# Moving four small steps of a gated-delta head loop: state products in two blocks, P on ScalarE, X ahead of the decays, z copied bank by bank

## The chip, the cores and the metric

The kernel runs on one NeuronCore of a Trainium2 chip. The metric is the device time of one execution in microseconds (us), lower is better. Before the change it is 2142.4 us, the median of three runs (2137.96, 2142.4 and 2145.52). The profiled execution is a fourth one, of 2137.08 us.

## The reference, cut to what matters

One step of a two-layer decoder over 320 tokens: 256 of a new prompt and 8 sequences with 8 new tokens each. Layer 1 is a gated DeltaNet mixer, layer 2 a pooling mixer; the change touches layer 1 alone. Its core, for 16 key heads with two value heads each:

```python
proj = h @ w_in                                   # 2048 x 12352: q, k, v, z, gates
qkv, conv_new = causal_conv(qkv, conv_buf, conv_w)   # width 4, then silu
q = l2norm(q) * HEAD_DIM ** -0.5;  k = l2norm(k)
# in chunks: S_t = exp(g_t) S_{t-1};  S_t += beta_t k_t (v_t - S_t^T k_t)^T;  o_t = S_t^T q_t
lmat = einsum('cd,ed->ce', kb, k) * decay_strict
tmat = triangular_solve(lmat + eye, eye)          # (1 + L)^-1, unit lower triangular
u = tmat @ (v * beta) - (tmat @ (kb * exp(gc))) @ s
o = (q * exp(gc)) @ s + (qk * decay_incl) @ u
s = s * exp(g_last) + kdec.T @ u
out = (rmsnorm(o, o_norm_w) * silu(z)) @ w_out
```

## The kernel before, in words

Everything is float32. A projection product is made of three fp32r matmuls: each weight and each activation is split into a high part (ScalarE, line 282, `whi`) and a remainder (VectorE, line 287, `wlo`), and `k_tile` (lines 290 to 298) multiplies high by high, high by low and low by high. A call of `k_tile` handles one tile of 128 rows of the inner dimension for two blocks of 128 output columns: six matmuls with 320 columns. A piece of weights has 4 such tiles; four slots hold pieces, SyncE loads them.

Layer 1 runs as a loop over heads with a software pipeline. Turn i does the attention-like work of head i-1 (`delta`, in each engine's part) and, between its many small products, the projection of head i: 48 tiles in three jobs of 16, job 0 for q and k (PSUM banks 0 and 1), job 1 for v (banks 2 and 3), job 2 for z (banks 0 and 1 again). TensorE's small products go to banks 4 to 7, named D0 to D3. Where TensorE's code says `fill(n)`, n projection tiles are issued: they are there to cover the time in which another engine answers. There is no scheduler. The order on each engine is the order of the code; engines meet at semaphores (`wait_ge`, `then_inc`). The loop has 15 turns (i from 1 to 15), and the sixteenth head runs behind it with tiles of the output projection as fill.

The inverse (1 + L)^-1 is built by doubling. Level k (1 to 5, `TILE_LEVELS`) makes two products, both in 32 x 32 blocks: one of L and Y (its end is `lp{k}`), which another engine copies out of PSUM as P (`pc`, or `p5` at level 5), and one of X and P (`lxt`), which ScalarE copies out as Y (`yc`, ended by `y{k}`), and VectorE turns into X (`xc`, line 1037). Level 5 joins 16 to 32 rows, a sixth level 32 to 64 (`p6`, `ym`, ended by `lp6`, `xt6`, `y6`). Y's full form `ym` is put together by GpSimd (line 551) once `y4` is there. GpSimd also scales the states (line 549) after the state products. The state products (line 1317) are 64 matmuls of 128 x 32 weights (`kq_m`, masked k and q) with the cached states `s_s` of the 8 sequences; they go to D3.

Beside that VectorE runs the convolution of head i (`conv_next`, line 937), the exponents of the next head's decays (`decays_next`, line 946), and the splits. ScalarE copies the projections out of PSUM: `qk_evac`, `v_evac` (lines 627 and 628), `z_evac` (line 635, into `zraw`), and saves the convolution's last rows (`cc_tail`, line 652). In the loop `v_evac` and `cc_tail` follow the eighth split, at level 4. At the end of a turn TensorE turns the head's output (`turned`, line 1290) and the next turn's first fill may start only when z has been copied, since it writes banks 0 and 1. The engines also wait for each other's round marks at the head of `delta` (`rounds`).

## Time and profile before

| | |
|---|---|
| three runs | 2137.96, 2142.4, 2145.52 us |
| profiled execution, its span | 2137.08 us, 2135.4 us |
| TensorE busy | 97% of the span, 19533 matmuls |
| VectorE, ScalarE, GpSimd busy | 1317.4, 842.4, 252.1 us |
| granted clock, mean | 0.99 |
| DMA | 311.40 MB, 146 GB/s |

Times of rows are microseconds from the start of the span, durations of one instruction are in ns where a row says mean. A busy TensorE is not one at its peak, since the ends of matmuls are modelled and matmuls overlap: the distance of two starts says what a matmul costs, not its duration. The clock is the share that was granted, 1.00 for 2.4 GHz. The head loop lies between about 111 and 1065 us.

### The profile page before, as it was taken

What the parts mean: (1) busy time and instruction counts of PE and PEld (TensorE: products, weight loads), DVE (VectorE), ACT (ScalarE), POOL (GpSimd) and SP (SyncE); (2) the same over time, 40 slices, a digit from 0 to 9 for tenths busy, and PEclk for the clock granted to TensorE, in tenths of its full rate; (3) what the DMA queues carried; (4) which work ended last, traced back from release to release, by engine and by line L of the source; (5) the groups of instructions that cost most, each with busy time, mean ns of one, the idle gap of its engine ahead of it and who ended that gap; (6) DMA issues with size and microseconds to landing.
All of it is one profiled execution on the core that took longest, in us unless ns stands there. A gap on an engine that the chain in (4) does not pass through costs nothing.

```text
span 2135.4 us, 51389 instructions
## 1 busy us (share of the span) xinstructions
PE 2073.1 (97%) x19533; PEld 1980.2 (93%) x19533; DVE 1317.4 (62%) x2203; ACT 842.4 (39%) x1674; POOL 252.1 (12%) x354
## 2 busy tenths in 40 slices
PE   6999999999999999999999999999999999999998
PEld 4889998989999999998889999999999999999997
DVE  4567777666777677677755444555555556654443
ACT  3444443434444434444443333433333333333333
POOL 3022121121121222112110010000000000000010
PEclk9999999999999999999999999999999999999999
DMA  5545544455453455545356445544444454444442
GB/s 162 148 117 148 148 141 129 118 149 148 133 163 113 134 163 146 153 132 150 117 156 192 138 143 173 158 146 149 159 154 146 155 162 156 146 152 150 157 140 88
DMA packets 379995, 311.40 MB, mean 146 GB/s; under 512 B 19609, under 2 KB 375866, under 8 KB 379322
## 3 DMA queue, kind: packets, MB, share of 16 engines
q1 hardware_dynamic: 378042, 306.30, 47.5%
q10 hardware_dynamic: 1872, 3.96, 0.5%
q8 instruction: 58, 0.95, 0.2%
q14 instruction: 23, 0.19, 0.0%
HBM read 283.85 MB, written 27.25 MB: 146 GB/s over the span
## 4 chain that ended last, share of the span: by engine, by line
PE 90%; DVE 5%; issue 3%; ACT 1%; DMA 0%; DVEq 0%; SPq 0%; ACTq 0%
PE ps L296 27%; PE ps L298 25%; PE ps L297 25%; PE ps L1153 8%; PE ps L1317 1%; DVE wlo L287 1%; DVE dec L946 1%; DVE convout L937 1%; PE ps L1174 1%; DMA xtok<-in_x_sample_dram 0%; ACT zraw L635 0%; DVE sq L843 0%; PE ps L1223 0%; PE ps L1267 0%; DVE s_s L1086 0%
## 5 line engine op out<-in xcount | busy, mean ns | idle before, releaser
L296 PE MATMUL ps<-xhi,whi 128*128 128x320 f32 x3072 | 995.1, 324 | 16.9 <-ACT zraw L635 7.4
L298 PE MATMUL ps<-xhi,wlo 128*128 128x320 f32 x3072 | 954.6, 311 | 2.3 <-issue 2.3
L297 PE MATMUL ps<-xlo,whi 128*128 128x320 f32 x3072 | 954.2, 311 | 2.7 <-issue 2.7
L287 DVE TENSOR_TENSOR wlo<-wraw,whi 128x1024 fp32r<-128x1024 f32 (+1 forms) x484 | 615.6, 1293 | 230.7 <-ACT whi L282 228.0
L296 PEld LDWEIGHTS ps<-xhi,whi 128*128 128x128 f32 x3072 | 581.4, 189 | 41.0 <-issue 32.9
L282 ACT ACTIVATE whi<-wraw 128x1024 fp32r<-128x1024 f32 (+1 forms) x484 | 495.6, 1049 | 262.6 <-PE ps L298 236.7
L298 PEld LDWEIGHTS ps<-xhi,wlo 128*128 128x128 f32 x3072 | 580.6, 189 | 6.0 <-issue 6.0
L297 PEld LDWEIGHTS ps<-xlo,whi 128*128 128x128 f32 x3072 | 581.8, 189 | 0.8
L298 PE MATMUL ps<-bhi,wlo 128*128 128x320 f32 x512 | 158.2, 309 | 0.0
L297 PE MATMUL ps<-blo,whi 128*128 128x320 f32 x512 | 158.2, 309 | 0.0
L296 PE MATMUL ps<-bhi,whi 128*128 128x320 f32 x512 | 158.1, 309 | 0.0
L1486 POOL TENSOR_TENSOR sacc<-sacc,sqp 128x640 f32<-128x640 f32 x12 | 18.9, 1575 | 942.9 <-ACT sqp L1509 942.9
L937 DVE SCALAR_TENSOR_TENSOR convout<-convin,cwcur,convout 128x344 f32<-128x344 f32 x192 | 102.0, 573 | 0.0
L1565 DVE TENSOR_TENSOR ht<-ps,ht 128x640 f32<-128x640 f32 x29 | 23.9, 825 | 122.3 <-PE ps L298 86.8
L298 PEld LDWEIGHTS ps<-bhi,wlo 128*128 128x128 f32 x512 | 96.2, 188 | 0.0
L296 PEld LDWEIGHTS ps<-bhi,whi 128*128 128x128 f32 x512 | 96.2, 188 | 0.0
L297 PEld LDWEIGHTS ps<-blo,whi 128*128 128x128 f32 x512 | 96.2, 188 | 0.0
L992 DVE SCALAR_TENSOR_TENSOR lmat<-ps,cur,dec 128x128 f32<-128x128 f32 x80 | 22.2, 344 | 101.4 <-PE ps L1153 101.4
L296 PE MATMUL ps<-phi,whi 128*128 128x320 f32 x256 | 78.9, 308 | 0.0
L297 PE MATMUL ps<-plo,whi 128*128 128x320 f32 x256 | 78.9, 308 | 0.0
L298 PE MATMUL ps<-phi,wlo 128*128 128x320 f32 x256 | 78.9, 308 | 0.0
L728 ACT ACTIVATE yc<-ps 128x64 f32<-128x64 f32 (+1 forms) x48 | 11.0, 229 | 159.2 <-PE ps L1153 159.2
(338 smaller groups left out, 2171.9 us busy)
## 6 DMA issues: line engine op xcount, KB each, us to landing
wraw<-in_delta_w_in_dram SPq DMA_DIRECT2D x384, 256.0 KB, 3.2
wraw<-in_pool_w_in_dram SPq DMA_DIRECT2D x256, 256.0 KB, 3.1
wraw<-in_delta_w_out_dram SPq DMA_DIRECT2D x128, 256.0 KB, 3.3
wraw<-in_pool_w_out_dram SPq DMA_DIRECT2D x128, 256.0 KB, 3.2
s_s<-in_state_delta_dram SPq DMA_DIRECT2D x32, 512.0 KB, 6.3
out_dram<-s_s SPq DMA_DIRECT2D x32, 512.0 KB, 5.0
wraw<-in_pool_w_group_dram SPq DMA_DIRECT2D x64, 256.0 KB, 3.1
dec<-gc_rows SPq DMA_DIRECT2D x16, 320.0 KB, 5.0
```

What stands on the lines that cost most here:

```text
L282: nc.scalar.activation(whi[:, slot, 0:width], wraw[:, slot, 0:width], ACT.Copy).then_inc(E("w_hi"), 1)
L287: nc.vector.tensor_tensor(wlo[:, slot, 0:width], wraw[:, slot, 0:width], whi[:, slot, 0:width].bitcast(F32), ALU.subtract).then_inc(E("w_l ...
L296: mm(o, whi[:, slot, w], hi[:, k_x, :], start=first, stop=False)
L297: mm(o, whi[:, slot, w], lo[:, k_x, :], start=False, stop=False)
L298: done = mm(o, wlo[:, slot, w], hi[:, k_x, :], start=False, stop=last)
L937: ins = v.scalar_tensor_tensor(convout[:, q, :], convin[:, q, j:j + CV], cwcur[:, q, j:j + 1], convout[:, q, :], ALU.mult, ALU.add)
L946: last = v.scalar_tensor_tensor(dec[:, u, :], dec[:, u, :], gc_next[:, u:u + 1], mask_p[:] if u < 4 else mask_s[:], ALU.add, ALU.add)
L992: last = v.scalar_tensor_tensor(lmat[:, u, :], D0[:, P * (u % 2 if u < 4 else 2):P * (u % 2 if u < 4 else 2) + P], cur[:, NBETA + u:NBETA ...
L1153: return mm(out, lhsT, rhs, start=True, stop=True)
L1174: mm(ps[:, 0, 0:T], ones[:], sq[:, q % 4, :], start=q == 0, stop=False).then_inc(E("sq_used"), 1)
L1317: last = mm(D3[32 * j:32 * j + 32, 256 + P * m:384 + P * m], kq_m[:, at:at + 32], s_s[:, 4 * h + b, q, :], start=b == 0, stop=b == 3)
L1565: v.tensor_tensor(tiles, ps[:, 2 * (j % 2):2 * (j % 2) + 2, 0:T], tiles, ALU.add).then_inc(E(f"free{j % 2}"), 1)
```

## The change

Four things, all in layer 1.

1. State products (TensorE): the one block of 64 at level 2, behind the fill of that level, becomes two of 32 (`states_part`): one behind the X-P product of level 1, one behind that of level 2. There they stand in the place of `fill(1)`. The two tiles go to the fills ahead of the X-P products, and one more tile goes there from the fill of 8 ahead of the normalized keys, which becomes 7.
2. P of level 5: ScalarE instead of VectorE copies it (`p5`), and then does its eighth split. The copy of v moves from level 4 behind the level-5 copy of Y, the convolution's last rows behind P6.
3. X: VectorE turns Y of level 4 before it computes the next head's decay exponents, not after. The copies of X into `xm` still come behind these, and the eighth split on VectorE behind the third such copy. TensorE waits for `x4` by name, since P no longer comes from the same engine.
4. z: the last two tiles of job 2 are multiplied bank by bank, with a signal (`z_half`) when bank 0 is complete, and ScalarE copies each bank when it is complete. For head 0 z is now copied within `silus`, ahead of the sample copies.

```diff
-    def k_tile(slot, k_w, hi, lo, k_x, pair, first, last):
+    def k_tile(slot, k_w, hi, lo, k_x, pair, first, last, halves=(0, 1)):
...
-        for h in range(2):
+        for h in halves:
...
         def z_evac(i, used):
-            act.wait_ge(E("w_used"), used)
+            act.wait_ge(E("z_half"), i + 1)
             if loop_of(i):
                 act.wait_ge(E("gate"), i)
-            sc.activation(zraw[:], ps[:, 0:2, 0:T], ACT.Copy).then_inc(E("z_evac"), 1)
+            sc.activation(zraw[:, 0, :], ps[:, 0, 0:T], ACT.Copy)
+            act.wait_ge(E("w_used"), used)
+            sc.activation(zraw[:, 1, :], ps[:, 1, 0:T], ACT.Copy).then_inc(E("z_evac"), 1)
...
-            if loop_of(i):
-                z_evac(i, i * 12 + (HEADS + 12))
+            z_evac(i, i * 12 + (HEADS + 12))
             act.wait_ge(E("silu"), i + 1)
...
+                if k == TILE_LEVELS:
+                    act.wait_ge(E("lp5"), n)
+                    sc.activation(p5[:], blocks(D0[:, 0:P], 4), ACT.Copy).then_inc(E("p5"), 1)
+                    split(8)
                 act.wait_ge(E("lxt"), (n - 1) * 5 + k)
...
-                if k < 5:
+                if k < 4:
                     split(4 + k)
+            v_next()
             act.wait_ge(E("lp6"), n)
             sc.activation(p6[0:64, :, :], blocks(D0[0:64, 0:256], 4), ACT.Copy).then_inc(E("p6"), 1)
+            tail_next()
             split(9)
...
         silus(0)
-        z_evac(0, HEADS + 12)
...
-                if j == 8:
-                    v_evac(i, i * 12 + (HEADS + 8))
-                    cc_tail(i)
...
-                    v.tensor_copy(p5[:], blocks(D0[:, 0:P], 4)).then_inc(E("p5"), 1)
                     dve.wait_ge(E("x4"), n)
...
-                if k == 4:
-                    decays_next()
                 if k < TILE_LEVELS:
                     dve.wait_ge(E("c_all"), 1)
                     dve.wait_ge(E(f"y{k}"), n)
                     turned = v.transpose(xc[:, 0:units, :], yc[:, 0:units, :])
                     if k == TILE_LEVELS - 1:
                         turned.then_inc(E("x4"), 1)
+                        decays_next()
...
-                last = k_tile((p // PK) % 4, k % PK, xhi, xlo, k, job % 2, k == 0, k == KT - 1)
+                slot = (p // PK) % 4
+                if job < 2 or k < KT - 2:
+                    last = k_tile(slot, k % PK, xhi, xlo, k, job % 2, k == 0, k == KT - 1)
+                elif k == KT - 1:
+                    for h in range(2):
+                        for kk in (KT - 2, KT - 1):
+                            last = k_tile(slot, kk % PK, xhi, xlo, kk, job % 2, False, kk == KT - 1, (h,))
+                        if h == 0:
+                            last.then_inc(E("z_half"), 1)
...
-            fill(8)
+            fill(7)
...
+            def states_part(part):
+
+                if part == 0:
+                    pe.wait_ge(E("kq_m"), n)
+                    pe.wait_ge(E("state_landed"), n * 32)
+                for b in range(4):
+                    for j in range(4):
+                        h, q = j % 2, j // 2
+                        at = (2 * part + h) * P + 32 * b
+                        last = mm(D3[32 * j:32 * j + 32, 256 + P * part:384 + P * part], kq_m[:, at:at + 32],
+                                  s_s[:, 4 * h + b, q, :], start=b == 0, stop=b == 3)
+                if part == 1:
+                    last.then_inc(E("ksqs_ps"), 1)
...
-                fill((2, 1, 2, 3, 2)[k - 1])
-                if k == 2:
...
-                    last.then_inc(E("ksqs_ps"), 1)
+                fill((3, 2, 3, 3, 2)[k - 1])
                 x = x0 if k == 1 else xc
                 pe.wait_ge(E("ident"), 1)
+                if k == TILE_LEVELS:
+                    pe.wait_ge(E("x4"), n)
                 pe.wait_ge(E(f"p{k}"), n)
...
-                if k < TILE_LEVELS:
+                if k < 3:
+                    states_part(k - 1)
+                elif k < TILE_LEVELS:
                     fill(1)
```

On TensorE, in the loop at levels 1 to 3, the rows before, from the L-Y product of level 2 to that of level 3 (`xhi,whi` and its two like are a fill tile's matmuls):

```order
L1153 MATMUL ps<-yc,lmat 32x16 [waits y1,ident]
L1153 MATMUL ps<-yc,lmat 32x16 x19
L296 MATMUL ps<-xhi,whi 128x320
...
L1317 MATMUL ps<-s_s,kq_m 32x128 [waits state_landed]
L1317 MATMUL ps<-s_s,kq_m 32x128 x31
L1153 MATMUL ps<-pc,xc 32x16 [waits p2,ident]
L1153 MATMUL ps<-pc,xc 32x16 x19
L296 MATMUL ps<-xhi,whi 128x320
...
L1153 MATMUL ps<-yc,lmat 32x16 [waits y2,ident]
```

and in the changed kernel, from the X-P product of level 1 to the L-Y product of level 3:

```order
L1156 MATMUL ps<-pc,x_100 32x32 [waits p1,ident]
L1156 MATMUL ps<-pc,x_100 32x32 x19
L1310 REGISTER_ALU [waits kq_m]
L1315 MATMUL ps<-s_s,kq_m 32x128 [waits state_landed]
L1315 MATMUL ps<-s_s,kq_m 32x128 x15
L1156 MATMUL ps<-yc,lmat 32x16 [waits y1,ident]
...
L1156 MATMUL ps<-pc,xc 32x16 [waits p2,ident]
L1156 MATMUL ps<-pc,xc 32x16 x19
L1315 MATMUL ps<-s_s,kq_m 32x128 x16
L1156 MATMUL ps<-yc,lmat 32x16 [waits y2,ident]
```

A state block now stands directly between two small products, without a fill on either side.

On VectorE, in the loop at levels 4 and 5, before (`p_82` is P of level 5, `dec` the decays of the next head):

```order
L1014 COPY_PREDICATED pc<-level,ps 128x4x16 [waits lp4,c_all]
...
L946 SCALAR_TENSOR_TENSOR dec<-dec,gc_next,mask_p 128x128 [waits hidden,dec_landed]
L946 SCALAR_TENSOR_TENSOR dec<-dec,gc_next,mask_p 128x128 x3
L946 SCALAR_TENSOR_TENSOR dec<-dec,gc_next,mask_s 128x128
L1037 STREAM_TRANSPOSE xc<-yc 128x128 [waits y4,c_all]
L1018 COPY p_82<-ps 128x128 [waits lp5,c_all]
L1020 COPY xm<-xc 32x4x32 [waits x4]
```

and in the changed kernel:

```order
L1018 COPY_PREDICATED pc<-level,ps 128x4x16 [waits lp4,c_all]
...
L1038 STREAM_TRANSPOSE xc<-yc 128x128 [waits y4,c_all]
L947 REGISTER_ALU
L950 SCALAR_TENSOR_TENSOR dec<-dec,gc_next,mask_p 128x128 [waits hidden,dec_landed]
L950 SCALAR_TENSOR_TENSOR dec<-dec,gc_next,mask_p 128x128 x3
L950 SCALAR_TENSOR_TENSOR dec<-dec,gc_next,mask_s 128x128
L1023 COPY xm<-xc 32x4x32 [waits x4]
```

The turning of X has passed the five exponents, and P's copy has left the engine.

On ScalarE, at the same place, before (`p_92` is P6):

```order
L728 ACTIVATE yc<-ps 128x4x16 [waits lxt]
L281 REGISTER_ALU [waits w_landed2]
L282 ACTIVATE whi<-wraw 128x1024 [waits w_used]
L627 ACTIVATE convin<-ps 128x2x256 [waits conv,w_used]
L628 ACTIVATE convin<-ps 128x2x8x8
L652 ACTIVATE tail<-convin 128x4x24 [waits v_evac,qk_evac,cc_o]
L654 ACTIVATE tail<-convin 128x4x3
L729 REGISTER_ALU
L732 ACTIVATE ym<-ps 32x4x32 [waits ym,lxt]
L732 ACTIVATE ym<-ps 32x4x32
L737 ACTIVATE p_92<-ps 64x256 [waits lp6]
```

and in the changed kernel:

```order
L733 ACTIVATE yc<-ps 128x4x16 [waits lxt]
L727 ACTIVATE p_82<-ps 128x128 [waits lp5]
L281 REGISTER_ALU [waits w_landed2]
L282 ACTIVATE whi<-wraw 128x1024 [waits w_used]
L729 REGISTER_ALU
L737 ACTIVATE ym<-ps 32x4x32 [waits ym,lxt]
L737 ACTIVATE ym<-ps 32x4x32
L627 ACTIVATE convin<-ps 128x2x256 [waits conv,w_used]
L628 ACTIVATE convin<-ps 128x2x8x8
L743 ACTIVATE p_92<-ps 64x256 [waits lp6]
L654 ACTIVATE tail<-convin 128x4x24 [waits v_evac,qk_evac,cc_o]
```

The copies of v (`convin`) now lie between the Y copies of level 5 and P6, and the tail behind P6.

## Rows read from the trace of the kernel before

**Rows 1.** The page, busy time of each engine over the span.

```profile
PE 2073.1 (97%) x19533; PEld 1980.2 (93%) x19533; DVE 1317.4 (62%) x2203; ACT 842.4 (39%) x1674; POOL 252.1 (12%) x354
```

**Rows 2.** Who waited for whom, TensorE: us in total, times, longest.

```profile
PE ps L296 <- ACT zraw L635: 7.4, 13, 3.5
PE ps L1153 <- DVE p L1018: 7.0, 13, 0.6
PE ps L296 <- issue: 5.8, 2, 3.0
```

**Rows 3.** Timelines of SyncE and TensorE (start, us, instruction), and the states' tile.

```profile
506.48 1.03 SPq L347 DMA_DIRECT2D s_s<-in_state_delta_dram  x2
...
526.76 0.41 PE L296 MATMUL ps<-xhi,whi 128*128 128x320 f32 x1
...
527.84 1.95 PE L1317 MATMUL ps<-s_s,kq_m 128*32 128x128 f32 x64
529.72 0.53 PE L1153 MATMUL ps<-pc,xc 32*32 32x16 f32 x40
...
531.62 0.41 PE L296 MATMUL ps<-xhi,whi 128*128 128x320 f32 x1
...
533.57 0.44 PE L1153 MATMUL ps<-pc,xc 32*32 32x16 f32 x32
...
L1317 PE MATMUL ps<-s_s,kq_m x64: 272/273/297, 527.8 to 529.5; 128*32 128x128 f32 x64
```

**Rows 4.** Three turns by window: length, engines busy, granted clock, DMA share, GB/s.

```profile
300.41:363.03 62.62, 61.73 (x773) 57.05 (x771) 46.28 (x93) 27.28 (x72) 13.01 (x12) 1.00 0.50 144
363.03:433.13 70.10, 64.49 (x774) 59.28 (x773) 45.13 (x93) 27.33 (x72) 12.80 (x12) 0.95 0.46 130
433.13:501.03 67.90, 63.62 (x773) 58.59 (x771) 46.21 (x93) 27.27 (x72) 13.25 (x12) 0.97 0.47 134
```

**Rows 5.** Timelines of ScalarE, GpSimd, VectorE and TensorE at levels 4 and 5.

```profile
538.73 0.22 ACT L728 ACTIVATE yc<-ps 128x64 f32<-128x64 f32 x1 [3.46 <-PE ps L1153]
...
539.03 1.82 POOL L551 TENSOR_TENSOR ym<-yc,blocks 128x640 f32<-128x640 f32 x1 [4.60 <-ACT yc L728]
...
539.37 2.43 DVE L946 SCALAR_TENSOR_TENSOR dec<-dec,gc_next,mask_p 128x128 f32<-128x128 f32 x4
...
541.98 0.30 DVE L1037 STREAM_TRANSPOSE xc<-yc 128x128 f32<-128x128 f32 x1
...
542.61 0.34 PE L1153 MATMUL ps<-p,xc 32*32 32x32 f32 x11 [0.56 <-DVE p L1018]
```

**Rows 6.** ScalarE's timeline from the copy of v to P6.

```profile
541.20 0.60 ACT L627 ACTIVATE convin<-ps 128x512 f32<-128x512 f32 x1 [1.30 <-PE ps L298]
541.69 0.28 ACT L628 ACTIVATE convin<-ps 128x128 f32<-128x128 f32 x1
...
544.91 0.38 ACT L737 ACTIVATE p<-ps 64x256 f32<-64x256 f32 x1 [1.28 <-PE ps L1153]
```

**Rows 7.** Timelines of TensorE and ScalarE at the end of a turn.

```profile
501.03 0.71 PE L1290 MATMUL ps<-ident,amat 128*128 128x128 f32 x5
...
501.23 0.70 ACT L635 ACTIVATE zraw<-ps 128x640 f32<-128x640 f32 x1 [4.37 <-PE ps L298]
...
502.06 0.41 PE L296 MATMUL ps<-xhi,whi 128*128 128x320 f32 x1 [0.33 <-ACT zraw L635]
```

**Rows 8.** Timelines ahead of the loop's first turn, and the window behind it.

```profile
106.86 0.76 ACT L679 ACTIVATE silu<-convout 128x688 f32<-128x688 f32 x1
...
109.12 0.86 DVE L960 SCALAR_TENSOR_TENSOR silu<-silu,convout 128x688 f32<-128x688 f32 x1
...
110.63 0.68 ACT L635 ACTIVATE zraw<-ps 128x640 f32<-128x640 f32 x1
...
111.45 0.41 PE L296 MATMUL ps<-xhi,whi 128*128 128x320 f32 x1 [3.46 <-ACT zraw L635]
...
111.40:116.60 5.20, 5.15 (x24) 5.16 (x25) 2.69 (x6) 2.53 (x4) 0.15 (x1) 0.67 0.50 147
```

More of the change, by code:

```diff
@@ L690, in branch_hi, with delta @@
             sc.activation(xhi[:, 4 * ch:4 * ch + 4, :], branch[:, 4 * ch:4 * ch + 4, :], ACT.Copy).then_inc(E("b_hi"), 1)
-        def delta(n, split, cached, store, next_silus, begun):
+        def delta(n, split, cached, store, next_silus, begun, v_next, tail_next):
             begun()
@@ L787, in split @@
                     qk_evac(i, i * 12 + (HEADS + 4))
-                if j == 8:
-                    v_evac(i, i * 12 + (HEADS + 8))
-                    cc_tail(i)
-            delta(i, split, lambda i=i: cc_evac(i), lambda i=i: cc_store(i), lambda i=i: silus(i), lambda: None)
+            delta(i, split, lambda i=i: cc_evac(i), lambda i=i: cc_store(i), lambda i=i: silus(i), lambda: None,
+                  lambda i=i: v_evac(i, i * 12 + (HEADS + 8)), lambda i=i: cc_tail(i))
         def out_split(j):
@@ L802, in delta_act @@
         branch_hi(0)
-        delta(NH, out_split, lambda: None, lambda: None, lambda: None, out_begun)
+        delta(NH, out_split, lambda: None, lambda: None, lambda: None, out_begun, lambda: None, lambda: None)
     def delta_dve(dve):
@@ L1010, in delta @@
                 units = 5 if k < S_LEVELS else 4
-                dve.wait_ge(E("c_all"), 1)
-                dve.wait_ge(E(f"lp{k}"), n)
                 if k < TILE_LEVELS:
+                    dve.wait_ge(E("c_all"), 1)
+                    dve.wait_ge(E(f"lp{k}"), n)
                     v.copy_predicated(half_blocks(pc[:, k - 1, 0:units, :], k, 1),
@@ L1021, in delta @@
                     v.tensor_copy(xm[BL:64, :, BL:64], xc[BL:64, 0:4, :])
-                split(3 + k)
-                if k < 5:
+                if k < TILE_LEVELS:
+                    split(3 + k)
                     conv_next(0, k - 1)
@@ L1042, in delta @@
                     v.tensor_copy(xm[BL:64, :, 0:BL], blocks(D2[BL:64, 0:P], 4)).then_inc(E("x5"), 1)
+                    split(8)
             conv_next(1, 0)
@@ L1307, in delta @@
                 last.then_inc(E(f"lp{k}"), 1)
-                fill((2, 1, 2, 3, 2)[k - 1])
-                if k == 2:
-                    pe.wait_ge(E("kq_m"), n)
-                    pe.wait_ge(E("state_landed"), n * 32)
-                    for m in range(2):
-                        for b in range(4):
-                            for j in range(4):
-                                h, q = j % 2, j // 2
-                                at = (2 * m + h) * P + 32 * b
-                                last = mm(D3[32 * j:32 * j + 32, 256 + P * m:384 + P * m], kq_m[:, at:at + 32],
-                                          s_s[:, 4 * h + b, q, :], start=b == 0, stop=b == 3)
-                    last.then_inc(E("ksqs_ps"), 1)
+                fill((3, 2, 3, 3, 2)[k - 1])
                 x = x0 if k == 1 else xc
                 pe.wait_ge(E("ident"), 1)
+                if k == TILE_LEVELS:
+                    pe.wait_ge(E("x4"), n)
                 pe.wait_ge(E(f"p{k}"), n)
```

## The prediction

> **What bounds the kernel now.** I read the page first, then who waited for whom on TensorE, then one turn of the head loop as a timeline, engine by engine. TensorE is busy for 2073.1 us of a span of 2135.4 us [rows 1], so only three things can pay: idle time of TensorE, matmul work that goes away, and time at the lower clock. In the list of waits two of the causes that the change touches stand out: the copy of z out of PSUM (7.4 us in 13 waits, the longest 3.5) and the copy of P at level 5 (7.0 us in 13 waits, never over 0.6) [rows 2]. A third cost is not a wait and stands in no list: what TensorE loses where projection matmuls change to the small matmuls of the heads and back. The timeline of starts shows it. A fill of one projection tile (six matmuls) reaches from 526.76 to 527.84, 1.08 us; one of two tiles from 531.62 to 533.57, 1.95 us [rows 3]. So a tile is worth 0.87 to 0.88 us and a fill costs 0.20 us more for being a piece of its own.
>
> A regular turn takes 62.6 us at full clock; two of the fifteen take 70.1 and 67.9 us [rows 4]. In both TensorE stood about 3 us at the turn with nothing named as releaser (5.8 us in two waits) [rows 2] and then had a lower granted clock (0.95 and 0.97 in the turn's mean).
>
> **State products.** The 64 products go from one block into two of 32. The first start is at 527.8, the last at 529.5, the next small matmul starts at 529.72 [rows 3]: 0.027 us each and some 0.2 us until the following block can start. Two blocks are 2 x (32 x 0.027 + 0.18) = 2.08 us against 1.88, so +0.2 (bounds: 0 if the drain overlaps, 0.4 if a block also has to be entered). Two one-tile fills between the small blocks disappear into longer fills elsewhere: 2 x 0.20 = -0.4. Net -0.2 per head, 16 heads: **-3.3 us** (bounds 0 and -6.4). Each half must cover what the fill covered, the copy of Y by ScalarE. Its like at level 4 starts right after the products end and takes 0.22 us [rows 5]; with 160 columns say 0.3. A half of 1.04 us hides that with about half a microsecond to spare. The fills before P get one tile more, so those covers only grow; the tile comes from the fill of 8, behind which normalized k is long ready. The states are needed about 2.6 us earlier, near 525.2; their loads were issued from 506.48 on [rows 3], over 17 us before, so I take that at 0.
>
> What the Trainium skill says here ("TensorEngine Tiling (Array Packing)", Key Properties): changing the tiling mode, not merely the tile, drains TensorE. The rows agree that there is such a cost, 0.20 us per break. Counted by the rule alone, this stretch has nine changes of mode before and six after, and at half a break each that would be -0.3 per head where my sum has -0.2; it also says that splitting the block is not free, which a count of instructions would miss.
>
> **P of the 16-to-32 level, and X.** In the loop the order on VectorE is: level-4 P, weight split, convolution, exponents of the next head's decays, X turned, P copied. The exponents begin at 539.37 and X is turned only at 541.98, 2.6 us for five instructions, because GpSimd's assembly of Y runs from 539.03 for 1.82 us; then P is copied, and the product starts at 542.61 after 0.56 us of idle TensorE [rows 5]. With the change ScalarE copies P when its product is done (near 540.2) and X is turned at 539.4, when the convolution ends. TensorE's two fill tiles end near 542.0. Both are ready 1.5 us earlier than that, so the wait goes: 7.0 us in all [rows 2], less some 0.3 of the last head, where VectorE is held by a residual addition that stays ahead of X: **-6.7 us** (bounds 0 and -7.0). Decays are now after X and still meet GpSimd; they end near 542 and the copies of X behind them near 542.8, while the product that needs them starts 3 us after the level-5 one. Covered; without cover this would cost at most the 0.6 just won.
>
> ScalarE pays by order: z aside, the v evacuation moves from before the level-5 copy of Y to behind it, ahead of P6. It takes 0.60 + 0.28 us [rows 6]. The Y copy would end near 542.8, v near 543.7, and P6 may start when its product ends, near 544.1 in the new time (before: 544.91 [rows 6], less the 0.8 us won in the turn). So 0.4 us of slack; the tail copy (0.5 us) then goes behind P6 and pushes the next weight split, and Y6 behind it, by about 0.1 us with a fill of one tile as cover. I take 0; if it is not covered it costs up to 0.3 per head, 5 us.
>
> **z bank by bank.** Before, the copy of 640 columns starts at 501.23, 0.70 us long, behind the last z matmul; TensorE has only five transposes from 501.03 and resumes at 502.06 after 0.33 us idle [rows 7]. After, half is copied while the other half is multiplied. A copy of 320 columns lies between 256 (0.38 us) and 512 columns (0.60 us) [rows 6], 0.44 us, so release comes 0.26 us earlier. Twelve clean turns: **-3.2 us** (bounds 0 and 12 x 0.33 = -4.0). The matmuls are the same, only the order of the last two k tiles differs.
>
> The first head has more. There z was copied behind the sample copies, which wait for VectorE's silu (from 109.12): z at 110.63, TensorE resumes at 111.45 after 3.46 us idle, and in the following 5.2 us the granted clock is 0.67, a mix of 2.4 and 1.2 GHz [rows 8]. Now z comes right behind the tanh, which ends at 107.6, and the last z matmul, which ended at 111.45 - 3.46 = 108.0: release near 108.6, -2.8 us. The 24 matmuls of the first fill then took 5.2 us [rows 8] where four tiles of 0.88 are 3.5; with an idle gap of under 1 us, as short as those at which no turn lost clock, this 1.5 us and more should not come. GpSimd's mark of the round, its one instruction of the window, comes after 111.4 [rows 8]; TensorE's fill would end at 108.6 + 3.6 = 112.2, just behind it. Sum **-4.3 us** (bounds -1 if the marks come late, -4.5).
>
> **Sum.** -3.3 - 6.7 - 3.2 - 4.3 = -17.5 us. The profiled execution took 2137.1 us (span 2135.4), giving 2119.6. The other runs are 2138.0, 2142.4 and 2145.5; the difference within these is about one disturbed turn. Off the median of 2142.4 I get 2124.9; off the mean of the four (2140.8) 2123.3. I say 2123.
>
> **Rivals.**
> A, the waits come back as others (chance 0.14): v before P6 or Y6 costs 0.3 per head and the first head stays bound by the round marks. -17.5 + 5 + 3.3 = -9, 2132 us. For it: ScalarE's queue grows denser exactly where TensorE needs four answers within 5 us. Against it: each has slack in the rows as worked out above.
> B, no net gain (0.09): the changes of tile mode around two state blocks cost 0.4 more than I have, and X or P is again late: only z remains, -3 to -5, 2138 us.
> C, slower (0.06): the turn of the loop. TensorE's disturbed turns cost 70.1 - 62.6 = 7.5 and 67.9 - 62.6 = 5.3 us, mean 6.4 [rows 4]. If the moved code makes them more frequent, from 2.7 additional ones (17.5 / 6.4) the gain is gone, from 4 on it is slower by over 0.3%; with five more, 2142.4 - 17.5 + 32 = 2157 us. For it: the same code has both kinds of turn, so it hangs on timing. Against it: the body grows by two instructions on TensorE, and the runs before vary by only one disturbed turn.
> The Trainium skill ("Runtime: NRT & Kernel Launch", Instruction fetch mechanics) says that a taken branch to code outside the fetched window stalls for a fetch. By that rule every turn or none should stall; the trace has it in two of fifteen.
> D, one or both disturbed turns vanish (0.09): 2123 - 6 to - 13, 2110 to 2117 us.
> The forecast itself has 0.62, its own range 2117 to 2129.
>
> **Range and chances.** 2109 to 2137 takes in D and A and part of B. A kernel that runs between 2138 and 2145.5 by itself shows a change of about 0.3% (6.4 us) and more. Faster: 0.62 + 0.14 + 0.09 = 0.85; within 0.3%: 0.09; slower: 0.06.
>
> **What would show it.** In the waits of TensorE the P rows must vanish (no row for P by either engine over 0.1 us) and the z row fall to about 1 us plus under 1 us once. In the timeline a turn takes 62.6 - 0.6 - 0.26 - 0.2 = 61.5 us. The two state blocks take 1.0 to 1.1 us each. The first head loop's F matmuls begin near 108.6, at full clock. Wrong would be: a regular turn of 62.3 us or more, a new wait of TensorE for P6, Y6 or X, VectorE's exponents reaching past the product that needs x5, or more than three turns of 67 us or longer.

## The result, and the profile after

The changed kernel took 2109.3 us (median of six executions, 2104.7 to 2114.2) against 2144.7 us for the kernel before (six executions on the same chip, 2138.0 to 2152.2): ratio 0.983, 95% interval 0.981 to 0.986. The difference of the medians is 35.4 us. I had 2123.0 with a range of 2109 to 2137, a gain of 17.5 to 19.4 us. So the direction was right, the time is at the low end of the range, and the size was half of what these runs show. The profiled executions differ by less, 22.9 us, and that difference can be followed line by line. Five of the executions used below (four of the kernel before, one of the kernel after) are over 1.5% slower than the fastest of their group and count as slow; without them the difference of the means given further down is 29.2 us instead of 27.7.

The page of the kernel after, span and busy times, answers to [rows 1]:

```profile
span 2112.4 us, 51389 instructions
PE 2064.3 (98%) x19533; PEld 1973.4 (93%) x19533; DVE 1335.2 (63%) x2187; ACT 845.7 (40%) x1706; POOL 254.5 (12%) x354
```

TensorE is busy for 8.8 us less. The other 14 us were idle time. Who waited for whom on TensorE (us in total, times, longest), against [rows 2]:

```profile
PE ps L296 <- issue: 5.7, 2, 2.9
PE ps L1650 <- DVE xn L1610: 3.9, 1, 3.9
PE ps L296 <- DVE xlo L956: 3.5, 1, 3.5
```

There is no row for P and none for z any more; only the first row, the wait without a releaser, still stands as before, 5.7 us in two waits.

Turns of the head loop by window (length, engines busy, granted clock of TensorE, DMA share, GB/s), against [rows 4]; the first is a regular one, then the two disturbed ones, then the last head, outside the loop:

```profile
662.66:724.15 61.49, 61.43 (x774) 56.95 (x772) 47.46 (x92) 27.47 (x74) 13.37 (x12) 1.00 0.51 146
724.15:791.93 67.78, 64.57 (x774) 59.60 (x771) 47.06 (x92) 27.47 (x74) 13.01 (x12) 0.95 0.48 134
791.93:860.84 68.91, 63.24 (x773) 58.40 (x771) 46.12 (x92) 27.47 (x74) 13.24 (x12) 0.98 0.46 132
1045.30:1109.78 64.48, 60.67 (x766) 56.39 (x765) 43.81 (x76) 28.94 (x69) 11.07 (x10) 1.00 0.53 167
```

The last head of the kernel before in the same view:

```profile
1064.97:1132.60 67.63, 63.39 (x766) 58.92 (x764) 42.58 (x77) 28.93 (x68) 11.07 (x10) 0.95 0.51 159
```

A regular turn went from 62.62 to 61.49 us. TensorE is idle in it for 0.06 us, where it was for 0.89. "Disturbed" means, here and below, a turn that is over 4 us longer than the regular ones. The 22.9 us of span are made up of

| stretch (start of one turned block to the next) | before | after | difference |
|---|---|---|---|
| up to the first head's turned block | 175.14 | 170.77 | -4.4 |
| twelve regular turns | 12 x 62.65 | 12 x 61.49 | -13.9 |
| two disturbed turns | 70.09 + 67.91 | 67.78 + 68.91 | -1.3 |
| last head | 67.63 | 64.47 | -3.2 |
| everything after it | 1002.8 | 1002.7 | -0.1 |

The three edits can be found one by one in a regular turn, by the distances of starts. From the L-Y product of level 1 to that of level 3 it was 8.90 us and is 8.66 (state products, -0.24). From the L-Y product of level 5 to the product behind it, which waits for P and X, it was 2.96 and is 2.32 (P and X, -0.64). From the turned block to the next fill it was 1.03 and is 0.77 (z, -0.26). Together -1.14 us.

The timeline of TensorE at levels 1 and 2 of the delta inverse (start, us, instruction), against [rows 3]:

```profile
502.14 1.08 PE L1315 MATMUL ps<-s_s,kq_m 128*32 128x128 f32 x32
503.15 0.53 PE L1156 MATMUL ps<-yc,lmat 32*32 32x16 f32 x40
...
506.02 1.08 PE L1315 MATMUL ps<-s_s,kq_m 128*32 128x128 f32 x32
507.03 0.44 PE L1156 MATMUL ps<-yc,lmat 32*32 32x16 f32 x32
```

From the start of a state block to the following product it is 1.01 us each time, 2.02 together for 1.88 in one piece: +0.14, where I had +0.2. The products after them start on the spot, so each half covers the copy of Y.

The timelines of ScalarE, GpSimd, VectorE and TensorE at levels 4 and 5, against [rows 5, 6]:

```profile
515.24 2.38 DVE L941 SCALAR_TENSOR_TENSOR convout<-convin,cwcur,convout 128x344 f32<-128x344 f32 x2
515.39 0.22 ACT L733 ACTIVATE yc<-ps 128x64 f32<-128x64 f32 x1 [3.46 <-PE ps L1156]
515.69 1.56 POOL L551 TENSOR_TENSOR ym<-yc,blocks 128x640 f32<-128x640 f32 x1 [4.42 <-ACT yc L733]
516.80 0.28 ACT L727 ACTIVATE p<-ps 128x128 f32<-128x128 f32 x1 [1.19 <-PE ps L1156]
517.55 0.30 DVE L1038 STREAM_TRANSPOSE xc<-yc 128x128 f32<-128x128 f32 x1
517.78 1.09 DVE L950 SCALAR_TENSOR_TENSOR dec<-dec,gc_next,mask_p 128x128 f32<-128x128 f32 x4
518.64 0.34 PE L1156 MATMUL ps<-p,xc 32*32 32x32 f32 x10
...
519.58 0.58 ACT L627 ACTIVATE convin<-ps 128x512 f32<-128x512 f32 x1
520.05 0.26 ACT L628 ACTIVATE convin<-ps 128x128 f32<-128x128 f32 x1
520.94 0.38 ACT L743 ACTIVATE p<-ps 64x256 f32<-64x256 f32 x1 [0.62 <-PE ps L1156]
```

P stands in SBUF at 517.1 and X is turned at 517.85; the product that needs both starts at 518.64 without a wait. The four exponents of the decays take 1.09 us here and took 2.43 before: GpSimd's assembly (515.69 to 517.25) now lies beside the convolution instead, and that takes 2.38 us where it took 1.05 before:

```profile
538.39 1.05 DVE L937 SCALAR_TENSOR_TENSOR convout<-convin,cwcur,convout 128x344 f32<-128x344 f32 x2
```

So the cost of running beside the assembly was moved, not removed, and X is turned later for it. ScalarE is idle for 0.62 us ahead of P6, so the v copy that was moved there is hidden (I had 0.4 of slack).

ScalarE and TensorE at the end of a turn, against [rows 7]:

```profile
539.01 0.44 ACT L635 ACTIVATE zraw<-ps 128x320 f32<-128x320 f32 x1 [3.49 <-PE ps L298]
539.69 0.71 PE L1301 MATMUL ps<-ident,amat 128*128 128x128 f32 x5
539.89 0.44 ACT L637 ACTIVATE zraw<-ps 128x320 f32<-128x320 f32 x1 [0.44 <-PE ps L298]
540.46 0.41 PE L296 MATMUL ps<-xhi,whi 128*128 128x320 f32 x1
```

The second half of z is copied in 0.44 us, as estimated, and TensorE goes on at 540.46, 0.06 us after its own transposes have ended.

Ahead of the first turn, against [rows 8]: both copies of z and the window of the fill behind them:

```profile
108.29 0.42 ACT L635 ACTIVATE zraw<-ps 128x320 f32<-128x320 f32 x1
...
108.68 0.44 ACT L637 ACTIVATE zraw<-ps 128x320 f32<-128x320 f32 x1
...
107.90:112.50 4.60, 4.11 (x30) 4.03 (x29) 4.22 (x10) 2.94 (x9) 0.15 (x1) 1.00 0.69 194
```

z comes at 109.1 where it came at 111.3, and the fill runs at full clock (1.00) where it had 0.67.

### The profile page after: what moved, and what is told of

The parts are those of the page before. It is cut to its first block, busy times and chain, and to the rows that moved or that the text cites. A ratio compares the mean times of both kernels' runs of the same rounds, so it can differ in the third digit from the quotient of the medians.

```text
span 2112.4 us, 51389 instructions
## 1 busy us (share of the span) xinstructions
PE 2064.3 (98%) x19533; PEld 1973.4 (93%) x19533; DVE 1335.2 (63%) x2187; ACT 845.7 (40%) x1706; POOL 254.5 (12%) x354
## 4 chain that ended last, share of the span: by engine, by line
PE 95%; DVE 3%; issue 1%; DMA 0%; ACT 0%; SPq 0%; DVEq 0%; ACTq 0%
PE ps L296 28%; PE ps L298 26%; PE ps L297 26%; PE ps L1156 9%; PE ps L1315 2%; PE ps L1177 1%; DVE wlo L287 1%; DMA xtok<-in_x_sample_dram 0%; DVE sq L847 0%; PE ps L1301 0%; PE ps L1234 0%; PE ps L1278 0%; DVE s_s L1089 0%; PE ps L1227 0%; DVE xlo L841 0%
## 5 line engine op out<-in xcount | busy, mean ns | idle before, releaser
L287 DVE TENSOR_TENSOR wlo<-wraw,whi 128x1024 fp32r<-128x1024 f32 (+1 forms) x484 | 628.0, 1319 | 228.2 <-ACT whi L282 225.7
L941 DVE SCALAR_TENSOR_TENSOR convout<-convin,cwcur,convout 128x344 f32<-128x344 f32 x192 | 118.5, 659 | 0.0
```

The source lines that it names most:

```text
L287: nc.vector.tensor_tensor(wlo[:, slot, 0:width], wraw[:, slot, 0:width], whi[:, slot, 0:width].bitcast(F32), ALU.subtract).then_inc(E("w_l ...
L941: ins = v.scalar_tensor_tensor(convout[:, q, :], convin[:, q, j:j + CV], cwcur[:, q, j:j + 1], convout[:, q, :], ALU.mult, ALU.add)
```

## The experiments

There were twelve runs, in three groups, of eleven kernels (e4 and e8 repeat the two kernels compared, e12 repeats e7); the kernels of a group share the runs of the kernel before on their chip. "Level 5" below is the 16-to-32 level; turn times are read as above, from one turned block of TensorE to the next.

**e1: z as before.** The rest of the change stays.

```diff
         def z_evac(i, used):
-            act.wait_ge(E("z_half"), i + 1)
+            act.wait_ge(E("w_used"), used)
             if loop_of(i):
                 act.wait_ge(E("gate"), i)
-            sc.activation(zraw[:, 0, :], ps[:, 0, 0:T], ACT.Copy)
-            act.wait_ge(E("w_used"), used)
-            sc.activation(zraw[:, 1, :], ps[:, 1, 0:T], ACT.Copy).then_inc(E("z_evac"), 1)
+            sc.activation(zraw[:], ps[:, 0:2, 0:T], ACT.Copy).then_inc(E("z_evac"), 1)
...
```

> The changed kernel with z as before: one copy of 640 columns, no order by bank, and z of head 0 behind the sample copies. Theory 1 (the parts are worth what the steps of the prediction give, and what is measured above their sum comes from turns of the head loop in which TensorE stalls about 3 us at the jump back, 6 to 7.5 us each, and whose number differs from execution to execution): a clean turn is 61.49 + 0.27 = 61.75 us, the first head about 4.3 us longer, so +7.5 us on the changed kernel's 2109: 2117. Theory 2 (the parts interact, each saves more than its term): +12 us or more, with a clean turn above 61.9 us.

Measured: 2118.1 us (2108.4 to 2128.4, six), ratio to before 0.988 (0.983 to 0.993). Trace: regular turn 61.80 us, 0.31 more than with the change; the first turned block at 174.57 instead of 170.77. TensorE's waits have the row again:

```profile
PE ps L296 <- ACT zraw L635: 6.7, 13, 2.8
```

So z is worth 0.3 us per turn, as worked out, and some 4 us once; the second is less sure, since the first turned block of the unaltered changed kernel lay at 170.77 us in one trace and at 168.29 in the other (e4).

**e2: P, X, decays, v and tail copy as before.** The rest of the change stays.

```diff
-                if k == TILE_LEVELS:
-                    act.wait_ge(E("lp5"), n)
-                    sc.activation(p5[:], blocks(D0[:, 0:P], 4), ACT.Copy).then_inc(E("p5"), 1)
...
                 else:
+                    v.tensor_copy(p5[:], blocks(D0[:, 0:P], 4)).then_inc(E("p5"), 1)
...
+                if k == 4:
+                    decays_next()
```

> The changed kernel with P of level 5 copied by VectorE, X turned behind the decays' exponents, and the copies of v and of the convolution's last rows at their old places. Theory 1: a clean turn is 61.49 + 0.6 = 62.1 us, in all +7 us, 2116. Theory 2: +12 us or more; the other parts had brought the small products closer together, so that the wait would now be longer than the 0.6 us of before.

Measured: 2115.9 us (2109.6 to 2127.0), ratio 0.987 (0.983 to 0.991). Trace: regular turns 61.93 to 62.16 us, 0.44 to 0.67 more, and the waits show P:

```profile
PE ps L1154 <- DVE p L1019: 5.4, 13, 0.5
```

**e3: one state block as before.**

```diff
+                if k == 2:
+                    pe.wait_ge(E("kq_m"), n)
+                    pe.wait_ge(E("state_landed"), n * 32)
+                    for m in range(2):
...
-                if k < 3:
-                    states_part(k - 1)
-                elif k < TILE_LEVELS:
+                if k < TILE_LEVELS:
                     fill(1)
```

> The changed kernel with one block of 64 state products at level 2 and the fills as before. Theory 1: a clean turn is 61.49 + 0.2 to 0.3 = 61.7 to 61.8 us, +3 to +4 us, 2113. Theory 2: +8 us or more.

Measured: 2113.4 us (2103.8 to 2119.8), ratio 0.986 (0.982 to 0.990). Trace: regular turn 61.73 us, 0.24 more (I had 0.2). This trace has one disturbed turn, 68.88 us.

**e4: the change again, unaltered**, as the measure for the three above.

> The changed kernel once more, unchanged, as the mark for the three others and for a second trace of it. Theory 1: a clean turn is again 61.49 us, but the number or the place of the turns of 67 us and more differs from the first trace (turns 10 and 11 there), and the time moves with it. If the place and number are the same as in the first trace, what disturbs them is not chance and theory 1 has to be changed.

Measured: 2113.2 us (2099.3 to 2142.4), ratio 0.986 (0.981 to 0.992). The trace's regular turn is 61.47 us. Disturbed are the sixth and the tenth turn (67.35, 68.63); in the first trace of the same kernel they were the tenth and the eleventh:

```profile
414.17:475.64 61.47, 61.41 (x773) 56.94 (x772) 47.46 (x92) 27.52 (x74) 13.07 (x12) 1.00 0.51 146
475.64:542.99 67.35, 63.04 (x773) 58.07 (x772) 46.63 (x92) 27.51 (x74) 13.03 (x12) 0.97 0.47 135
```

The three parts, taken back one at a time, cost 0.31, 0.44 to 0.67 and 0.24 us of a turn, 0.99 to 1.22 together; the change as a whole won 1.14. They add up and don't hide one another. In the medians of six (2118.1, 2115.9, 2113.4, 2113.2) the order is the expected one but e3 can't be told from e4, and the six executions of e4 alone spread over 43 us (28 without the slowest).

**e5 and e6: TensorE's loop over the heads written out**, in the kernel after and in the one before. It takes away the jump back at the end of a turn, and leaves each turn's work as it is.

```diff
...
-        with pe.Fori(1, NH) as i:
+        for i in range(1, NH):
```

> The changed kernel with TensorE's head loop written out: its 15 turns stand one behind another, without a jump back; the other engines keep their loops, the work and the waits are the same. Theory 1 (the stalls of about 3 us belong to TensorE's jump back): no turn of over 63 us, all turns 61.5 us, the time 2100 us (the profiled span of 2112.4 less 6.3 and 7.4 us of its two disturbed turns, plus 1.7), and the executions lie within some 6 us of each other instead of 40. Rival (the stalls come from what TensorE waits for at a turn, z or the round marks, or from DMA traffic): disturbed turns stay as frequent. Rival 2: code now has to be fetched for every turn, and each turn gets its own short stalls, as in the first turn: all turns 1 us or more longer, 2115 us or more.

Measured e5: 2118.3 us (2111.7 to 2122.1), ratio 0.989 (0.985 to 0.993). No turn begins with a stall (the starts of the last transpose and of the next fill are 0.25 us apart at each), but turns take 61.39 to 65.17 us. So the stalls of about 3 us went with the jump back, as theory 1 had it, but the time is that of rival 2: TensorE has short stalls within the turns, and fourteen turns take 14.8 us more than at 61.39 us each. Three of them, and the rows of the DMA queue that brings code and of the waits:

```profile
168.01:233.18 65.17, 63.41 (x774) 58.67 (x772) 47.47 (x92) 27.50 (x74) 13.14 (x12) 0.97 0.50 139
...
298.24:360.96 62.72, 61.61 (x774) 57.04 (x772) 47.34 (x92) 27.51 (x74) 13.30 (x12) 1.00 0.50 144
360.96:422.35 61.39, 61.39 (x774) 56.92 (x771) 47.48 (x92) 27.51 (x74) 13.19 (x12) 1.00 0.52 147
...
q8 instruction: 126, 2.06, 0.4%
...
PE ps L1156 <- issue: 5.0, 7, 1.3
PE ps L1315 <- issue: 4.7, 4, 1.8
```

> The kernel before with TensorE's head loop written out in the same way. Theory 1: clean turns of 62.6 us throughout, 2124 us, and so a distance of 24 us to the changed kernel without its jump back; that distance is then what the four edits are worth, and the rest of the 35 us between the first medians is a different number of disturbed turns. If the distance stays at 30 us or more, the edits themselves are worth more than the traces show.

Measured e6: 2130.4 us (2127.8 to 2136.4, twelve), ratio 0.995 (0.992 to 0.997). Turns 62.56 to 66.23 us. The spread over twelve executions is 8.7 us, where the looped kernel before spread over 35 us in 23 executions of the same job, and over 38 us in the twelve of e8. That shows where most of the spread comes from: the jump back. The written-out loop trades the 3 us stall for short ones within the turns.

The two written-out kernels are only 12.1 us apart by their medians, where 24 were expected, and 17.0 us in the traces (spans 2127.0 and 2110.0). Their undisturbed turns differ as before, 62.56 and 61.39 us, but the short stalls cost the changed kernel more: 14.8 us over fourteen turns against 9.0. The trace of e5 is its fastest execution (2111.7 us), so in the others the stalls may have cost more still; no trace shows it. What the change is worth thus depends on how the loop's code is fetched, and 24 us hold for the looped kernels alone.

**e7: TensorE waits for z bank by bank too.** In the change ScalarE copies by banks but TensorE waits for both.

```diff
-            sc.activation(zraw[:, 0, :], ps[:, 0, 0:T], ACT.Copy)
+            sc.activation(zraw[:, 0, :], ps[:, 0, 0:T], ACT.Copy).then_inc(E("z_first"), 1)
...
-                if job < 2 or k < KT - 2:
+                if job == 0 and k == 0 and not isinstance(i, int):
+                    k_tile(slot, 0, xhi, xlo, k, 0, True, False, (0,))
+                    pe.wait_ge(E("z_evac"), i)
+                    last = k_tile(slot, 0, xhi, xlo, k, 0, True, False, (1,))
+                elif job < 2 or k < KT - 2:
```

> The changed kernel with z released to TensorE bank by bank: the first product of the next turn waits for the copy of bank 0 only, and for bank 1 only ahead of its second half. In the trace of the changed kernel 0.30 us of a turn are still lost behind the turned output (starts 0.33 us apart where 0.03 is the least). Theory: the distance falls to 0.03, a clean turn to 61.2 us, 15 turns make -4.5 us, the first head about -0.4 more: 2105 to 2108 by median, in the clean turns -0.3. Rival: the wait between the two halves costs as much as it saves, a clean turn stays at 61.5 us.

Measured: 2096.1 us (2094.6 to 2113.4), ratio 0.979 (0.975 to 0.983), the lowest of all and below the 2105 to 2108 expected (the same kernel gave 2105.3 in e12). The trace's regular turn is 61.16 us, with the gap between the transposes and the next fill down to 0.03 us:

```profile
307.85:369.01 61.16, 61.16 (x774) 56.92 (x772) 47.49 (x92) 27.50 (x74) 13.02 (x12) 1.00 0.52 146
```

**e8: the kernel before, unaltered**, twelve executions.

> The kernel before once more, for a second trace. Theory 1: clean turns of 62.6 us as in the first, another number or place of turns of 67 us and more; over its executions the number must be 3 or so in the mean, since the median lies some 20 us above the 2124 of a run without any.

Measured: 2143.2 us (2125.5 to 2163.8), ratio 0.998 (0.995 to 1.002). The trace (span 2149.8) has three disturbed turns, 72.05, 71.81 and 69.69 us, and its regular turn is 62.63 us as ever. What queue q8 carried, first for the kernel before in the first trace (two disturbed turns), then here (three), then for e3 (one):

```profile
q8 instruction: 58, 0.95, 0.2%
```

```profile
q8 instruction: 67, 1.10, 0.2%
```

```profile
q8 instruction: 49, 0.80, 0.2%
```

That is 40 packets and nine more for each disturbed turn. It held in all twelve traces of looped kernels: 49 with one, 58 with two, 67 with three, and one packet more (59 with two, 68 with three) in the two kernels below that have 128 matmuls more ahead of the loop. In the first trace of before the stretch of a disturbed turn, 363.03 to 433.13, has

```profile
q8 instruction: 9, 0.15, 1.0%
```

and a regular one (563.66 to 626.29) has no such row. So a disturbed turn is one in which code is fetched again; that it is TensorE's loop body follows from e5, where TensorE's loop alone is written out and no turn begins with the stall.

**e9: the kernel before with head 0's z copied early**, nothing else.

```diff
-            if loop_of(i):
-                z_evac(i, i * 12 + (HEADS + 12))
+            z_evac(i, i * 12 + (HEADS + 12))
...
-        z_evac(0, HEADS + 12)
```

> The kernel before with one edit: z of head 0 is copied ahead of the sample copies instead of behind them. Theory (the prediction's step): TensorE idles some 0.9 us ahead of the loop instead of 3.0 to 3.7, loses no clock there, and the first turn's output comes 3.5 to 4.3 us earlier; later turns stay at 62.63 us. About 2138 us by mean, if the number of disturbed turns stays the same as before. Rival: the round marks or the loads of the first weights hold the first head, and it gains under 1 us.

Measured: 2142.6 us (2120.1 to 2151.6, twelve), ratio 1.002 (0.999 to 1.005). In the trace TensorE resumes 1.0 us after its last start instead of 3.7 and the first turned block is at 171.74, 3.4 us earlier than in the first trace of the kernel before and 4.6 earlier than in e8. The local gain is there, but the times don't show it: the median is 4.7 us above that of the 29 executions of the kernel before in this job (2138.0), the mean 4.3 above (2141.1 and 2136.8). This trace has three disturbed turns (69.66, 71.57, 70.31).

**e10: a shift by 64 one-column products ahead of the loop**, in the kernel before. If the place of the loop's code, or the moment at which the loop starts, decided how many turns are disturbed, this would change their number. In the trace each of the 64 calls has become two matmuls with a weight load each, so there are 128 more matmuls (19661), not 64.

```diff
         pe.wait_ge(E("cc_out"), 1)
+        for _ in range(64):
+            one(D2[:, 0:1], ident[:], ones[:, 0:1])
         one(D2[:, 0:1], ident[:], ones[:, 0:1]).then_inc(E("pe_round"), 1)
```

> The kernel before with 64 matmuls of one column, with their 64 weight loads, ahead of TensorE's head loop. They compute nothing that is used and lie in a stretch where TensorE waits for z anyway; they move the loop's code by 128 instructions. Theory (where the code lies sets how often the jump back ends in a stall): the number of disturbed turns changes clearly, the spread of the executions (2125 to 2165 so far, 0 to 6 disturbed turns of 6.5 us) becomes narrow, at 2124 to 2128 or above 2150. Rival (it is chance from one execution to the next, whatever the place): mean 2144, spread of 20 us or more, as without the shift.

Measured: 2163.1 us (2145.3 to 2181.6, twelve), ratio 1.011 (1.007 to 1.015). It looks like three more disturbed turns, and the trace says otherwise: there are three, as in e8, but the first turned block is at 193.82 us instead of 175.14. The added matmuls themselves, and the stretch at the lower clock:

```profile
106.58 22.89 PE L1153 MATMUL ps<-ones,ident 128*128 128x1 f32 x130
...
111.90:132.40 20.50, 20.50 (x95) 20.50 (x95) 2.19 (x6) 0.90 (x2) 0.15 (x1) 0.50 0.17 52
```

The one-column matmuls (130, with the two of the round mark that were there before) run without a pause from 106.58 to 129.3 us, 0.11 us from start to start until the granted clock falls at 111.9, and 0.21 us after that. The first fill begins at 129.34 instead of 111.45. So they did not fit into the wait for z, and the 18.7 us by which the first turned block is late are nearly all their own time. Less that, the median is 2144.4 us; e8's is 2143.2, the 29 executions of the kernel before in this job have 2138.0.

**e11 and e12: the same shift in the kernel of e7, and that kernel again.**

```diff
+        for _ in range(64):
+            one(D2[:, 0:1], ident[:], ones[:, 0:1])
```

> The kernel with z released bank by bank (clean turns of 61.16 us) with the same 64 small matmuls ahead of the loop. They do not all fit into the wait there, so up to 1.5 us are lost in the first head. Theory of the place of the code: another number of disturbed turns than without the shift (0 in four of six executions there), so 2096 or below with hardly a disturbed one, or 2110 and above. Rival (chance): as without the shift, most executions at 2096 to 2098 and one or two 6 to 13 us above.

Measured e11: 2133.3 us (2122.5 to 2148.1, twelve), ratio 0.998 (0.995 to 1.001). First turned block at 192.28, 24.3 us later than in e12 and 20.7 later than in e7 (171.61); the one-column matmuls again run from 106.61 to 129.4 us. Two disturbed turns. Neither of the two times expected, 2096 or 2110 and above, allowed for the some 20 us that the added matmuls take.

> The kernel with z released bank by bank once more. If the number of disturbed turns of a kernel is fixed by its code, it again has few: median 2095 to 2099. If it is chance, the executions spread over 2095 to 2120 as those of the changed kernel do (2099 to 2142), with clean turns of 61.16 us all the same.

Measured e12: 2105.3 us (2101.4 to 2129.2, six), ratio 0.987 (0.983 to 0.991). The trace (span 2099.6) has one disturbed turn. The same stretch as above, without the shift:

```profile
111.90:132.40 20.50, 20.50 (x279) 19.82 (x280) 12.89 (x33) 9.61 (x32) 3.53 (x6) 1.00 0.44 130
```

e7 and e12 are one kernel; their medians differ by 9 us and their regular turns by nothing (61.16). That the place of the code or the loop's starting moment sets the number of disturbed turns is not borne out by e10 and e11: their traces have three and two with the shift, as those without have three or two, and two or one. These are counts of one trace each.

## Why the prediction was right or wrong

**Right: the mechanisms, and what each is worth in a turn.** The P wait is gone, with P ready 1.5 us ahead of the product as I had it. X is ready only 0.8 us ahead, where I had 1.5 for it too: I expected GpSimd's assembly to meet the decays still, and it met the convolution ahead of X (2.38 us for 1.05). e2 prices this part at 0.44 to 0.67 us per turn for 0.56 to 0.6 forecast. Two state blocks cost 0.14 instead of 0.2, and e3 prices the part at 0.24 for 0.2. e1 prices z at 0.31 for 0.26. ScalarE's v, P6 and Y6 cost nothing, as forecast. The first head came 4.4 us earlier for 4.3, and both of its terms are in the trace: the distance of starts at the gap went from 3.71 to 0.74 us, and the clock of the fill from 0.67 to 1.00. That the sum fits to 0.1 us is luck: the same two kernels in e8 and e4 have their first turned block at 176.38 and 168.29 us, 8.1 apart. A regular turn takes 61.49 us where I wrote 61.5.

On the drain: that changing the tiling mode drains TensorE (the Trainium skill, "TensorEngine Tiling (Array Packing)", Key Properties) agrees with the rows. A block of 32 state products goes from its last start to the following product in 0.2 us, in two blocks as in one. But I counted the changes of mode wrong. From the L-Y product of level 1 to that of level 3 there are nine before and eight after, not six (31 and 30 over a whole turn). At half a break each that is -0.1 per head, where this stretch became 0.24 us shorter and e3 gives 0.24. The count of pieces did better: two fills of their own less, 2 x 0.20, and 0.14 more for the second state block, make -0.26.

**Wrong: the size of the sum.** Where it was short shows in the table above. First, the last head: my terms left it 0.3 us. Its stretch had another cost before that I hadn't read, TensorE idle for 4 us ahead of the fill and then a lower clock (0.95 over the stretch). After, the stall is nearly the same (3.99 and 3.78 us) but in this execution no clock was lost: -3.2. In the other traces of kernels with the change it was lost in part (65.95 us in e4, 66.52 in e2), and 64.47 is the lowest of the eight traces of looped kernels with the change (the others 65.95 to 66.94), where the four with the old code have 66.91 to 67.88. So half or more of the 3.2 is luck of the trace. Second, the three terms make 1.02 us of a regular turn (0.56 + 0.26 + 0.2), 12.2 over twelve, and they measured 13.9, 1.7 more: the P term most of all, for the list of waits holds only the 0.56 us of idle time and the stretch became 0.64 shorter; a few of the regular turns before were also up to 0.12 us longer than 62.63. Third, the disturbed turns together gave 1.3 for some 0.5; they vary by more than that from one to the next. That is 2.9 + 1.7 + 0.8, the 5.4 us between 17.5 and 22.9.

**Wrong: the step from one execution to the medians.** "The difference within these is about one disturbed turn", taken from four executions, was the step that failed most, and with it the choice to weigh rivals C and D at 0.06 and 0.09. Taking each trace's disturbed turns down to regular ones leaves 2135.4 - 12.7 = 2122.7 us of span before and 2112.4 - 13.7 = 2098.7 after, 24.0 apart (as times, with the 1.7 us around the span, 2124.4 and 2100.4). The second pair of traces, e8 and e4, gives 2124.2 and 2097.7 us of span in the same way, 26.5 apart. The times of 81 executions of the kernel before run from 2121.0 to 2164.7, the lowest near its undisturbed level. Eleven disturbed turns in the four traces of the kernel before, e9 and e10 among them, cost 7.6 us on average (5.3 to 9.4), so by this estimate an execution has between none and some five or six, not one more or less. The mean of these 81 is 2141.3 us; the twelve of the kernel after have 2113.6 us (2099.3 to 2142.4). The ratio of these means is 0.987, by resampling 0.984 to 0.990 (chips and jobs mixed): 27.7 us. The six executions behind the result were low ones (median 2109.3; the other six of the same kernel 2113.2), and those of before were the highest (2144.7; in other jobs 2142.7, 2139.1, 2143.2 for e8, and 2138.0). So of the 35.4 us some 24 to 26 are the edits; the rest I put down to the disturbed turns that each side happened to get, which the traces make likely but can't show for executions without one. Six executions of the kernel before, drawn at random from the 81, have a median that itself varies by 4.1 us (one standard deviation), three by 6.2. My bound of 0.3% for what can be told from no change was too small for this kernel with so few executions; e9 shows it, where the first head is over 3 us earlier in the trace and the median of twelve is 4.7 us above the base.

**Rivals.** A didn't come: no wait took the place of P or z. B neither; its extra 0.4 for mode changes isn't there (e3). C isn't seen: the looped kernels with the change, whole or in part, have one to three disturbed turns in the trace, those with the old code two or three. D, fewer disturbed turns, happened to the measured sample without being the change's doing as far as these runs can tell. The means over all executions give, as an estimate, (2141.3 - 2124.4) / 7.6 = 2.2 disturbed turns before and (2113.6 - 2100.4) / 6.4 = 2.1 after, 6.4 us being the mean of the fifteen in the traces with the change. The traces themselves have 11 in four (2.8 each) with the old code and 15 in eight (1.9 each) with the change, and the mean of the twelve executions after is uncertain by some 3 us, half a turn. So a small difference in number is neither shown nor excluded, and D stays open.

On the jump back, the Trainium skill ("Runtime: NRT & Kernel Launch", Instruction fetch mechanics) says that a taken branch outside the fetched window stalls. The traces agree that such a stall is one of fetching (nine packets each), and e5 and e6 that it goes with the branch. But in most turns the same branch costs nothing, where the page's rule would have every turn or none stall. In which turns it comes stays open, since no run here tells what decides it.

## What to carry to other kernels

Read each turn of a loop apart, and compare regular turns with regular turns: three edits of 0.2 to 0.6 us per turn were sized to 0.1 or 0.2 us that way, where medians of six couldn't separate one of them. Ask the trace before you call something small: the 64 calls of e10 and e11 were meant to fit into a wait and took 22.8 us. If some turns of one trace are disturbed at random, collect many executions before taking a median as a base, and give the range the spread of that count. Copy a PSUM result out bank by bank and let both ends, the copy and the next writer, wait by bank: the copy alone gave 0.3 us per turn, the writer's wait another 0.3 (e7).

## What the runs showed of the hardware that I had not expected

- Jumping back to the head of a long loop on TensorE is free in most turns, which fetch no code, and costs 4.6 to 9.4 us in others, which fetch nine packets of 16 KB. Over the 26 such turns in the twelve traces the mean is 6.9 us. TensorE stands 2.3 to 3.0 us at the turn (mean 2.6) and for 2.3 us more, on average, in further short stalls without a releaser in the same turn; the lower granted clock takes 2.4 us on average, counted as the missing share of the clock over the turn, some of which falls into idle time (in two of the 26, one of e1 and one of e2, it stayed at 1.00). Which turns these are changes between executions of one kernel. Written out, the loop costs up to 3.8 us per turn in short stalls instead, and the kernel before becomes steady (8.7 us of spread over twelve executions).
- One-column matmuls are not cheap when each has its own 128x128 weights to load: 128 of them, from 64 calls, took 22.8 us, 0.11 us each at 2.4 GHz and 0.21 at 1.2. The granted clock fell to 0.50 at 111.9 us while they ran without a pause, 5.3 us after the first, and rose again at 132.4, 3.1 us after the projection matmuls had begun, in both kernels with them; without them it is 1.00 over that stretch in e12.
- A stall of 3 to 4 us may or may not lower the clock: at the last head 3.78 us cost nothing in the trace of the change, and 1.5 us of the following fill in e4, where it was just as long.
- VectorE beside GpSimd's assembly: the four exponents took 2.43 us beside it and 1.09 without, two steps of the convolution 2.38 beside it and 1.05 without.
